# The rotary swap as transfers, and attention's first pair inside the last group of the input projection

## The reference

```python
def apply_rope(x, cos, sin):
    x1, x2 = xf[..., 0::2], xf[..., 1::2]
    y = jnp.stack([x1 * c - x2 * s, x1 * s + x2 * c], axis=-1).reshape(x.shape)
q = apply_rope(rms_norm(heads(z[0]), p['g_q_a']), cos, sin)
w = jax.nn.softmax(jnp.concatenate([s_lat, s_ctx], axis=-1), axis=-1)
```

## Time and profile before

| | us |
|---|---|
| median of three runs | 1823.34 |
| lowest, highest | 1820.26, 1827.17 |
| the profiled execution | 1822.5 |
| its span | 1820.7 |
| mean granted clock of TensorE | 0.982 |
| busy: PE, DVE, ACT, POOL | 1701.0, 1179.1, 822.7, 267.4 |

### The profile page before, as it was taken

How to read it: one execution, slowest core, us unless ns; L and a number is a source line. 1 busy time by engine, 2 the same in 40 slices (tenths; PEclk the granted TensorE clock), 3 DMA queues, 4 the chain that set the end, 5 groups by cost and what they waited for, 6 DMA issues and landing times. The chain is left out here.

```text
span 1820.7 us, 29026 instructions
## 1 busy us (share of the span) xinstructions
PE 1701.0 (93%) x11838; PEld 1502.5 (83%) x11838; DVE 1179.1 (65%) x1684; ACT 822.7 (45%) x1244; POOL 267.4 (15%) x212
## 2 busy tenths in 40 slices
PE   6999999989898999999999989999898989999998
PEld 4778897768778999899999868878677788989897
DVE  6373637667438797886987966654767484747472
ACT  5433315646217534535435463232655283527161
POOL 0334623202100000000000033362311200000000
PEclk9999999989998999999999999999999989999999
DMA  9541112000346357257276033121200355536251
GB/s 384 163 165 47 48 47 113 27 1 2 118 159 262 135 181 308 98 207 312 69 288 231 23 122 107 70 105 59 116 2 1 116 200 217 204 143 253 95 185 47
DMA packets 43519, 247.19 MB, mean 136 GB/s; under 512 B 5604, under 2 KB 7050, under 8 KB 24714
## 3 DMA queue, kind: packets, MB, share of 16 engines
q1 hardware_dynamic: 43402, 245.55, 36.1%
HBM read 218.79 MB, written 26.74 MB: 135 GB/s over the span
## 5 line engine op out<-in xcount | busy, mean ns | idle before, releaser
L3456 PE MATMUL ps<-op_hi,w_hi 128*128 128x384 f32 x880 | 301.3, 342 | 20.5 <-DVE xT L2612 9.3
L866 POOL TENSOR_TENSOR w_lo<-raw,w_hi 128x512 fp32r<-128x512 f32 x124 | 174.4, 1437 | 962.8 <-ACT w_hi L1003 940.3
L3456 PE MATMUL ps<-op_lo,w_hi 128*128 128x384 f32 x880 | 298.2, 339 | 0.0
L3456 PE MATMUL ps<-op_hi,w_lo 128*128 128x384 f32 x880 | 298.1, 339 | 0.0
L1514 ACT ACTIVATE w_hi<-raw 128x1024 fp32r<-128x1024 f32 x96 | 101.6, 1060 | 200.0 <-PE ps L3456 140.3
L3456 PEld LDWEIGHTS ps<-op_hi,w_hi 128*128 128x128 f32 x880 | 167.2, 190 | 28.4 <-issue 16.6
L3456 PEld LDWEIGHTS ps<-op_lo,w_hi 128*128 128x128 f32 x880 | 167.4, 190 | 0.0
L3456 PEld LDWEIGHTS ps<-op_hi,w_lo 128*128 128x128 f32 x880 | 167.3, 190 | 0.0
L1450 ACT ACTIVATE w_hi<-raw 128x1024 fp32r<-128x1024 f32 x80 | 82.4, 1054 | 147.2 <-PE ps L3419 125.4
L3103 PE MATMUL ps<-w_hi,h_hi 128*128 128x256 f32 x448 | 131.9, 294 | 0.0
L2566 DVE TENSOR_TENSOR w_lo<-raw,w_hi 128x1024 fp32r<-128x1024 f32 x96 | 115.9, 1217 | 20.3 <-ACT w_hi L1514 20.1
(11 more groups left out here) (397 smaller groups left out, 3937.6 us busy)
## 6 DMA issues: line engine op xcount, KB each, us to landing
raw<-w_big SPq DMA_DIRECT2D x96, 1024.0 KB, 6.1
raw_m<-w_modl SPq DMA_DIRECT2D x21, 1024.0 KB, 5.8
op_hi<-op_cache SPq DMA_DIRECT2D x21, 768.0 KB, 4.7
op_lo<-op_cache SPq DMA_DIRECT2D x21, 768.0 KB, 6.2
raw<-w_modl SPq DMA_DIRECT2D x14, 1024.0 KB, 4.9
op_hi<-op_cache SPq DMA_DIRECT2D x21, 512.0 KB, 3.8
op_lo<-op_cache SPq DMA_DIRECT2D x21, 512.0 KB, 5.5
first_mod<-w_modl SPq DMA_DIRECT2D x8, 1024.0 KB, 21.1
```

Source lines behind the costliest of these rows:

```text
L866: ins = nc.gpsimd.tensor_tensor(w_lo[r][:, ks, :], src[:, ks, :], w_hi[r][:, ks, :].bitcast(F32), ALU.subtract)
L3456: ins = mm(bank(base + g, 0, h), wide(w)[:, k, g * P:(g + 1) * P], ops[hl][:, k, 0:h], start=(p in FRESH and k == 0 and q == 0), stop=(k = ...
```

## The change

- **Swap by transfers.** The matrix `gswap`, its making on DVE and the matmuls of `turn` are gone. ACT issues two transfers per feature ahead of its squares, one for the even and one for the odd partitions: 64 partitions of 512 floats each, 128 KB, from `ft[i]` to `st[i % 3]`. DVE's second product reads `st` in place of PSUM, with gains swapped in the same way (`gqk_swap`); the sign lies in the sine constants. It waits for both transfers.
- **The last group's bank.** Group 22 sums in bank 6, which the rotation has left free.
- **Pair 0 of attention.** Its scores are made in the middle of group 22, after the sixth `mean_squares`, once three features are normed and group 21 is copied out. DVE makes its maxima after step 46 and ahead of group 22's copy, ACT its exponentials ahead of the weight split. They go to `prob_first`, over `rab[0]` and `rab[1]`.
- **Waits.** PE waits for the sixth `qk_ready` ahead of the scores of pair 1 and for the last token group ahead of pair 0's transposes. SP waits also for pair 0's last transposes ahead of loading `xT` back.

The diff, cut to its core:

```diff
+    gqk_swap = keep("gqk_swap", [4])
...
-    gswap = place("gswap", mod_acc_at, [P])
-    st = [place(f"st{i}", RX + 5 * TB + i * 2048, [SEQ]) for i in range(2)]
+    st = [place(f"st{i}", RX + 5 * TB + i * 2048, [SEQ]) for i in range(3)]
+    prob_first = place("prob_first", RX, [2, T])
...
+    def swap_landed(l, i):
+        return slot_landed(3 + i % 3), 16 + 32 * (2 * l + i // 3 + 1)
...
+    def group_at(g, a, n):
+        return ps[:, 6 * 512 + a:6 * 512 + a + n] if g == len(GROUPS) - 1 else pair(g, a, n)
+    def prob_of(u):
+        return prob[u % 2] if u else prob_first
...
                 sp.wait_ge(sem("qk_ready"), 6 * (l + 1))
+                sp.wait_ge(sem("trb_done"), sum(len(key_span(m, j)[1]) > 2 for i in range(l) for m, j, _ in att_pairs(i)) + 1)
                 sp.dma_start(xT[:], x_keep.rearrange("p (k t) -> p k t", k=KD)).then_inc(sem("x_back"), 16)
...
                 if i >= 3:
                     act.wait_ge(sem("qk_ready"), 6 * l + i - 2)
+                for x in range(2):
+                    nc.scalar.dma_start(st[i % 3][x::2, :], ft[i][1 - x::2, 0:SEQ]).then_inc(swap_landed(l, i)[0], 16)
                 nc.scalar.activation(rab[i % 3][:, 0:n], ft[i][:, 0:n], ACT.Square).then_inc(sem("sqab_ready"), 1)
...
+                        if (s, m) == GROUPS[-1]:
+                            probs(l, 0, 0, T_("nba").n, T_("nbb").n)
+                            probs(l, 0, 1, T_("nba").n, T_("nbb").n)
                         if m == 1:
                             split_hi(l * PROJ + s + 2)
...
                         gla_step(l, q)
+                        if (s, m) == GROUPS[-1]:
+                            maxima(l, 0, 0, T_("sca").n, T_("scb").n, T_("exp").n)
+                            maxima(l, 0, 1, T_("sca").n, T_("scb").n, T_("exp").n)
...
-                if -1 <= i < 5:
-                    v.tensor_scalar(gswap[:], swap, gqk[:, G_OF[i + 1]:G_OF[i + 1] + 1], None,
-                                    ALU.mult).then_inc(sem("gswap_ready"), 1)
...
-                dve.wait_ge(sem("rot_done"), 6 * l + i + 1)
-                step(v.tensor_tensor(st[i % 2][:], bank(6 + i % 2), sin, ALU.mult))
-                v.tensor_tensor(rt[i % 3][:], rt[i % 3][:], st[i % 2][:], ALU.add).then_inc(sem("turned"), 1)
+                dve.wait_ge(*swap_landed(l, i))
+                step(v.scalar_tensor_tensor(st[i % 3][:], st[i % 3][:], gqk_swap[:, G_OF[i]:G_OF[i] + 1], sin,
+                                            ALU.mult, ALU.mult))
+                v.tensor_tensor(rt[i % 3][:], rt[i % 3][:], st[i % 3][:], ALU.add).then_inc(sem("turned"), 1)
...
-                    turn(l, q - PREP_AT)
                     mean_squares(l, q - PREP_AT)
...
-                mm(bank(6 + i % 2), gswap[:], ft[i][:, 0:SEQ], start=True, stop=True).then_inc(sem("rot_done"), 1)
...
                                 if j == j0 + n // 2 - 1:
                                     gla_step(l, 4 * s + 2 * m)
+                                    if (s, m) == GROUPS[-1]:
+                                        pe.wait_ge(sem("qk_ready"), 6 * l + 3)
+                                        pe.wait_ge(*evacuated(l, g - 1))
+                                        scores(l, 0, T_("exp").n)
...
-                pe.wait_ge(sem("qk_ready"), T_("qk").add(6))
-                pe.wait_ge(sem("vt_ready"), 10 * (l + 1))
...
-                scores(0)
                 for u in range(n):
                     if u + 1 < n:
-                        scores(u + 1)
+                        if u == 0 or pairs[u][0] != pairs[u + 1][0]:
+                            pe.wait_ge(sem("qk_ready"), 6 * (l + 1))
+                        scores(l, u + 1, e0)
+                    if u == 0:
+                        pe.wait_ge(sem("vt_ready"), 10 * (l + 1))
```

More of the change, by code:

```diff
@@ L102 @@
 LV_BG = 69
-LV = 71
+LV_GSW = 71
+LV = 75
 V_ALL = V_L + LV
@@ L1843, in norm, with maxima @@
                 T_("hf").add(KD)
+            def maxima(l, u, hb, sa0, sb0, e0):
+                m, j, p = att_pairs(l)[u]
+                lo, _, _ = key_span(m, j)
+                h = p + 2 * hb
+                ready = sem("nbb_ready" if hb else "nba_ready")
+                dve.wait_ge(*((sem("sca_done"), sa0 + u + 1), (sem("scb_done"), sb0 + u + 1))[hb])
+                if u >= 2:
+                    dve.wait_ge(sem("exp_done"), e0 + 2 * u - 2)
+                if m == 0:
+                    v.tensor_reduce(nb[:, u % 2, hb:hb + 1], bank(2 * hb, lo, T - lo), AX_X, ALU.max,
+                                    negate=True).then_inc(ready, 1)
+                else:
+                    step(v.tensor_reduce(mx[:, u % 2, hb:hb + 1], bank(2 * hb, lo, T - lo), AX_X, ALU.max,
+                                         negate=True))
+                    step(v.tensor_tensor(nb[:, u % 2, hb:hb + 1], mx[:, u % 2, hb:hb + 1], nsink[:, h:h + 1],
+                                         ALU.min))
+                    v.tensor_tensor(se[:, u // 2 % 2, 2 * p + hb:2 * p + hb + 1], nb[:, u % 2, hb:hb + 1], rowc[:, h:h + 1],
+                                    ALU.add).then_inc(ready, 1)
             def in_proj(l):
@@ L3059, in mean_squares, with scores @@
                 ins.then_inc(sem("msab_ready"), 1)
-            def turn(l, i):
-                if i == 0:
-                    pe.wait_ge(sem("yc_ready"), TILES * l + n_q(l) // P)
-                if i >= 2:
-                    pe.wait_ge(sem("turned"), 6 * l + i - 1)
-                pe.wait_ge(sem("gswap_ready"), 6 * l + i + 1)
-                pe.wait_ge(sem("ft_ready"), FEATS * l + 8 + i)
-                mm(bank(6 + i % 2), gswap[:], ft[i][:, 0:SEQ], start=True, stop=True).then_inc(sem("rot_done"), 1)
+            def scores(l, u, e0):
+                m, j, p = att_pairs(l)[u]
+                lo, keys, masks = key_span(m, j)
+                qf, kf = ft[3 * m + p], ft[3 * m + 2]
+                ra, rb = slice(0, 64), slice(64, 128)
+                if masks:
+                    for hb in range(2):
+                        if u >= 1:
+                            pe.wait_ge(sem("exp_done"), e0 + 2 * u - 1 + hb)
+                        for x_, (mk, at) in enumerate(masks):
+                            mm(bank(2 * hb, at, P), ident_b[:], mk[:], start=(x_ == 0), stop=False,
+                               skip_group_check=True)
+                elif u >= 1:
+                    pe.wait_ge(sem("exp_done"), e0 + 2 * u - 1)
+                ins_a = mm(bank(1, 0, CTX), qf[ra, cols(j)], kf[ra, SEQ:T], start=True, stop=True)
+                if u >= 1 and not masks:
+                    pe.wait_ge(sem("exp_done"), e0 + 2 * u)
+                if lo < 512:
+                    k0 = keys[0] * P
+                    mm(bank(2, lo, 512 - lo), qf[rb, cols(j)], kf[rb, k0:k0 + 512 - lo], start=not masks,
+                       stop=True, skip_group_check=bool(masks))
+                    ins_a = mm(bank(0, lo, 512 - lo), qf[ra, cols(j)], kf[ra, k0:k0 + 512 - lo],
+                               start=not masks, stop=True, skip_group_check=bool(masks))
+                ins_a.then_inc(sem("sca_done"), 1)
+                mm(bank(3, 0, CTX), qf[rb, cols(j)], kf[rb, SEQ:T], start=True, stop=True).then_inc(
+                    sem("scb_done"), 1)
             def in_proj(l):
@@ L3679 @@
         vrows.append(a["b_gla_gate"][l])
+        vrows += [np.tile(a[n][l].reshape(-1, 2)[:, ::-1].reshape(-1), 2)[None] for n in ("g_q_a", "g_k_a", "g_q_b", "g_k_b")]
         g = np.zeros((P, 2, P), np.float32)
```

100 lines of the change are left out of this document (27 added, 73 removed).

## The result

The changed kernel took **1804.51 us** (median; 1803.31 to 1806.09) beside 1823.05 us of the kernel before: ratio 0.9895, 95% interval [0.9875, 0.9916], that is 18.5 us less. The profiled execution has a span of 1802.2 us (1804.2 with what lies around it) where the one before had 1820.7.

The account below looks back on a forecast made before the run. PE (93% busy) was taken as the bound where full, with DVE's chain followed in the second layer. 7.7 (first layer) + 7.0 (second) - 2.1 (POOL) = 12.6 us less, so 1810.7 us; range 1805.5 to 1816.0.

Parts of the forecast that it names:

- Matmuls of the swap: First layer's projection: PE loses six swap steps of 0.86 us, all on the path, 5.2 us.
- Pair 0 inside group 22: First layer's start of attention: the boundary gives 4.1 us, less 1.6 for scores put into the last group.
- POOL and the gates: Behind the projection, DVE's gates' gain falls into POOL's weight split: 1.05 us lost per layer, 2.1 in all.
- Second layer: Projection's end to attention: DVE's chain starts earlier, ends at 1292.9, and pair 1's maxima come 7.0 us sooner.
- The transfers: Swap transfers in both layers: landing in 3 us, covered by about 7 us as a rule, 4.7 at tightest; no cost.
- The sum: Whole kernel: 7.7 + 7.0 - 2.1 = 12.6 us less, giving 1810.7 us.
- (a): Gates escape POOL and the second layer keeps its clock: 2.1 + 0.7 us more gained, 1807.9 us; chance 0.17.
- (b): The gain at attention's start is given back, only the swap matmuls count: 9.4 us gained, 1813.9 us; chance 0.15.
- (c): Products reading two SBUF operands meet POOL's splits and ACT's issues cost double: 7.7 us gained, 1815.6 us; chance 0.07.
- (d): Swap transfers land late and DVE waits: gain gone at about 8 us to landing, 1835 us at 9; chance 0.05.

Follow-up runs that it names:

- 416 bytes: The changed kernel with 416 bytes of unused space ahead of its activations, so they start at the old kernel's addresses: 1813.13 us, ratio 0.9942.
- before_moved: The kernel before, same instructions, with five small tiles (416 bytes) moved behind its activations, giving the changed kernel's addresses: 1821.65 us, ratio 0.998.
- the squares first: The changed kernel with each feature's square on ACT ahead of that feature's two transfer issues: 1803.19 us, ratio 0.9887.

## Why the prediction came out as it did

**Matmuls of the swap (right).** 5.2 us forecast in the first layer, 4.7 with the swap alone.

**Pair 0 inside group 22 (right, one size off).** PE waited 1.86 us as forecast, the exponentials of pair 0 were done, and pair 1's maxima came 4.55 us after the group, not 3.4: the scores ran at the lower clock level. With 416 bytes, and the full clock there, the 3.4 came. The lower level follows 1.86 us of an idle PE behind a full one; before, 1.78 us of idle time had stood there at a granted clock of 1.00, so it could not be read from the rows. Nor does it follow each time: with the 15 extra matmuls 1.86 us of idle time left the full clock. The stage gave 6.2 of 6.65.

**POOL and the gates (right in place, half right in kind).** In the first layer the gain paid 1.06 us. In the second it ran in the midst of POOL's split and paid nothing: 1.22 us for 1024 columns, as in the kernel before, where it ran clear of the split. There POOL paid: its four instructions took 5.96 us instead of 4.95. POOL's fourth add began at 313.26 in the first layer, just ahead of DVE's gain at 313.32, and took its usual 1.26; in the second it began at 1290.09, just behind DVE's at 1290.03, and took 2.28. Whoever comes second waits. The Trainium skill (SBUF — State Buffer, "SBUF: two separate sides") has it that the two exclude each other for a whole instruction; the rows agree, with 1.06 us for DVE here and 1.01 for POOL there. I had charged DVE both times.

**Second layer (right to a microsecond, by another way).** I followed DVE and put the issues at 0.33 each by SP's row. This step failed: on ACT a pair of issues takes 1.1 to 1.5 us, ACT with PE behind it became the chain (2.73 us of PE's waiting, 1 to 2 forecast), and from the fourth rotation to the last norm it took 16.65 us, not 13.7. Issues above 0.4 us with the squares late were one of the prediction's own signs of being wrong. What the issues cost of that is argued from the rows; no run took them off ACT with pair 0 in place. The stage gave 4.7 of 5.95 in the profiled execution, where PE ran at the lower level at pair 0's scores; in the two repetitions, whose traces have the full clock there, those 16.65 us were 15.0 and the stage gave 6.5. That it lies near 5.95 is in part luck: the rotations began some 2.0 us earlier against the work ahead of them, not 1.0, and this made up for part of the longer chain.

**The transfers (right).** They cost nothing once issued, and nothing waited for them. The estimate of about 2.6 us by the Trainium skill (DMA: Bandwidth & Descriptors, "Anatomy of one DMA — SWDGE (gpsimd) path") for the two halves, which the page's fit gives for another issuing path, is nearer to the 2.1 measured for one of them than the 3 that I took.

**The sum (the step that failed).** It adds up what the edit does to the two boundaries, and holds that nothing else moves. Two terms are missing. One is the last product: -4.1 us, of which before_moved shows that the start addresses bring 3.6. I had read that the swap matrix leaves the constants and gave it no price. The other is the clock in the first layer's windowed attention, three half-clock stretches before and none after: 3 x 1.1 = 3.3 of the 3.4 us measured. The prediction looked at the clock only at the second layer's boundary, and didn't count on it. With both, 12.6 + 4.1 + 3.3 = 20.0; less the start's 1.8, the two boundaries' 1.7 and plus twice 0.9 in between, 18.3, the difference of the two profiled executions. That is an account of two executions. Over the medians the last product's term repeats in every trace at these addresses (2.8 to 4.9 us), while the clock's may be smaller, as the mean clocks say.

**The rivals.** (a) *more* was nearest in number, for another reason. (b) fell: pair 0 alone gave its time. (c) and (d) fell: all twelve products with the sine took 0.74 us, and nothing waited for a transfer. One product with the cosine met POOL in each layer (1.78 and 1.75 us); before, one instruction met it in the first layer and two in the second, so these meetings didn't become more.

**What stays open.** What property of an address makes the matmuls faster (multiples of 64 don't; 105920 and 106368 bytes are fast, 105952, 105984 and 106336 slow), and which operand it concerns, wasn't found; the two stretches of 0.9 us neither. All three traces of the changed kernel as it is lack the half-clock stretches, and each of its eight variants (five of them moved in memory or time alone) has at least one, also the one with 15 more matmuls. But every kernel's clock varies between its executions, and one of each was traced (the three of the changed kernel at the highest clock, but the pad of 32 bytes and the squares first, with two stretches each, at 0.984 too), so whether the stretches go by the kernel, by the phase of the work or by the execution isn't shown. None of the versions beats the changed kernel beyond the intervals.

## What to carry to other kernels

A change that frees or adds constants moves every buffer behind them. Compare it at equal addresses (a pad of the freed size is one line) before its gain is credited to its instructions: here 18.5 us were some 11 of edit at the old addresses, and 8 of placement and clock. Compare also the mean clock of all executions before a difference in the clock of two traces is credited to a change. And when a DMA issue is put on a compute engine, don't price it by another engine's row; in the second layer here nothing waited for the landing, while the issue stood in the chain.

## What the runs showed of the hardware

- **Matmul pace and placement.** The same 128x512 f32 matmuls at the full clock follow each other every 228.1, 230.0, 233.3, 234.2 or 234.3 ns, by where the buffers start in SBUF (steps of 32 bytes suffice); 231.1 is a mixture, as at byte 105920 three of nine traces have one run of 192 at the slower pace (22.5 us for 96 matmuls, 22.1 otherwise). 32 bytes were worth some 17 us of 1805, of which some 11 in the two MLPs.
- **Issue of a transfer on ACT**, SBUF to SBUF, 64 partitions with a step of two, 2 KB each: 0.47 to 1.04 us, median 0.6; on SP one of another kind took 0.33. It can run beside an instruction of ACT (1261.96 to 1263.08, under a split). Landing 1.9 to 4.7 us, median 2.1.
- **A half-clock stretch in a stage that is a chain** costs about 1.1 us. The mean clock of one kernel's executions goes from 0.977 to 0.984, and its time from 1810 to 1802 us with it.
- **POOL and DVE reading SBUF side by side**: about 1.0 us for one meeting, paid by the one that comes second. With the squares first DVE's gain began (309.90) in POOL's third instruction and ran into the fourth: DVE took 1.94 us for 1.75, and POOL's fourth 2.78 for 1.26.
